# Retention queries and keys turned by DMA transposes of two 16-bit planes, in a two-layer decoder trunk

## The chip, the cores and the metric

The kernel runs on one core of a Trainium2 chip. The metric is the device time of the whole program in microseconds (us): the median of several runs, smaller is better. Beside the runs there is one profiled execution, whose trace lists every instruction of every engine: TensorE (PE in the rows; PEld are its weight loads), VectorE (DVE), ScalarE (ACT), GpSimd (POOL) and SyncE (SP; SPq is its queue of DMAs).

## What is computed

Two layers of a decoder trunk (`DEPTH = 2`), in float32, over 2048 prompt rows (16 tiles of 128) and 32 sample rows. Each layer has an attention head group (A) and a retention head group (B), whose outputs are gated, joined and projected back:

```python
h = rms_norm(x, norm_g);  p = einsum('ntd,de->nte', h, w_in)
qb = rotary(qb, pos, B_DK, theta_b);  kb = rotary(kb, pos, B_DK, theta_b) * B_DK ** -0.5
# retention, per chunk of 128 rows, B_HEADS = 4 heads, B_DK = B_DV = 128
scores = einsum('nihd,njhd->nhij', q, k) * decay
inner  = einsum('nhij,njhv->nihv', scores, v)
cross  = einsum('nihd,nhdv->nihv', q, S) * q_dec
S_new  = exp(lg * C) * S + einsum('njhd,njhv->nhdv', k * k_dec, v)
x = x + concat(silu(g_A) * A, silu(g_B) * rms_norm(inner + cross)) @ w_out
```

For `scores` and `cross` a product contracts over d, so the queries and keys of a tile, which lie in memory with one row of the sequence per partition, must be turned to have d on the partitions.

## The kernel before

A layer runs in four stages with the same 17 steps each, one per 128-row tile and one for the sample rows: A (projection of the attention columns, attention), B0 (projection and retention of heads 0 and 1), B1 (heads 2 and 3), O (the output projection). In the stages B0, B1 and O the steps are T0, T1, S (the sample rows), T2, 4, 5, ... up to F, the last one; a hardware loop runs most of them. The projections are float32 products made of three float16 products (high and low parts), 8 blocks of the contraction each. So one half of a step's projection (`proj`, L514) is 12 matmuls of 128x512, and a step has four such halves: two into one PSUM bank (queries and keys), two into the other (values and gate).

Each engine has a program of its own, written out in order; semaphores tie them together. In the stages B0 and B1 `step2` puts the retention of the tile before between the four halves of a tile's projection:

- after the first half: `b_T` (L657), four TensorE transposes of 128x128 float32 of the rotated queries and keys (`land[:, b, 0:512]`, two heads each) into PSUM bank `TK`;
- after the second: `b_ST` (L668), the scores, from `qkT`;
- after the third: `b_OS` (L687, L694, L703), outputs and state;
- after the fourth: nothing.

VectorE writes the rotated queries and keys in `b_rope` (L1162, L1170, L1171; it raises `b_qk`). It stands behind `b_decay` (L1182), which waits for the scores of the tile before. ScalarE copies the turned ones out of `TK` in `b_tout` (L1792, raises `b_te`, for which `b_ST` waits). It also makes the float16 weights of the next stage (`w_high`, L1657), the squares of the outputs (`b_squares`, L1799), and values and gate (`b_vg`, L1775 to L1779). SyncE's queue carries the mixed outputs to memory (`store_mix`, L2095), the sample states (`load_states`, L2110; stored at L2268), the DMA transposes of attention (`prob_T`, L2135), which turn 128x2048 numbers of float16 (512 KB) each, and in stage O those of the mixed rows (L2246) and of the next layer's input (L2252).

At the start of B0 the last attention tile, E, is still being worked on: `a_PV` of its two head groups stands after the third and the fourth half of B0's step T1, in front of `b_OS` of T0, and SyncE still has its two `prob_T` to issue.

Of the kernel before, what the change touches and what calls it, by code (L numbers as in the profile page):

```python
# [36 lines left out]
P = 128  # L37
# [133 lines left out]
def mid(c, i=0):  # L171

    return Step(c, i, SAMPLE_AT)
# [24 lines left out]
def trunk(nc, x_prompt, x_sample, cache_k, cache_v, state_ret, w_in, w_out, norm_g, q_g, k_g, sinks,  # L198
          rope_ap, rope_as, rope_bp, rope_bs, mask_a, mask_s, decay, decay_s, cols, ident,
          y_p, y_s, nk_p, nv_p, nst_p, nk_s, nv_s, nst_s, mixed):  # L200
    with ExitStack() as ctx:
# [70 lines left out]
        qkT = r2[:, 0:512]  # L272
        osq = r2[:, 640:896]
# [43 lines left out]
        b_qk, b_tk, b_te = sem("b_qk_ready"), sem("b_transposed"), sem("b_transposes_out")  # L317
# [58 lines left out]
        def all_h(eng, L):  # L376

            for p in range(2):
                eng.wait_ge(h_in[p], 16 * (L + 2) * (9 - p))

# [112 lines left out]
        def _(pe):  # L493
# [156 lines left out]
            def b_T(ph, L, s):  # L650

                b, r = lpar(ph, s), s.rows
                if ph == "B0" and s.fixed and s.c < 2:
                    pe.wait_ge(a_mx, 2 * (L + 1) * STEPS - 2 + 2 * s.c)
# [107 lines left out]
            def b_work(ph, L, s):  # L762
                return [[lambda: b_T(ph, L, s - 1)], [lambda: b_ST(ph, L, s - 1)],
                        [lambda: b_OS(ph, L, s - 1)], []]

            pe.wait_ge(id_ld, ID_LOADS * 16)
            def layer(L, last):
# [7 lines left out]
                with pe.Fori(0, (STEPS - 5) // 2) as i:  # L775
# [10 lines left out]
                    [lambda: b_T("B0", L, T0)],  # L786
# [3 lines left out]
                for ph in ("B0", "B1"):  # L790
# [5 lines left out]
                    b_T(ph, L, T1)  # L796
# [10 lines left out]
                step2("B1", L, F, [  # L807
                    [lambda: b_T("B1", L, F - 1)],
                    [lambda: b_ST("B1", L, F - 1)],
                    [lambda: b_OS("B1", L, F - 1)],  # L810
                    [lambda: b_T("B1", L, F)]])
# [837 lines left out]
        def _(act):  # L1649
# [132 lines left out]
            def b_tout(ph, L, s):  # L1782
                act.wait_ge(b_tk, bn(ph, L, s) + 1)
                if s.sample:
                    A.activation(qkT[:, 0:4 * NS], TK[:, 0:4 * NS], ACT.Copy)
# [81 lines left out]
            def layer(L, last):  # L1867
# [76 lines left out]
                F = mid(STEPS - 1)  # L1944
                b_vg("B0", L, T0)
                b_tout("B0", L, T0)
                b_vg("B0", L, T1)
                b_squares("B0", L, T0)

                def b_step(ph, s, k=None):  # L1950
                    nxt = "B1" if ph == "B0" else "O"
                    b_tout(ph, L, s - 1)
                    if k is not None:
                        w_high(L, nxt, k, 0)
                    b_squares(ph, L, s - 1)
# [4 lines left out]
                for ph in ("B0", "B1"):  # L1960
                    if ph == "B1":
                        b_tout("B0", L, F)
                        b_squares("B0", L, F)
# [6 lines left out]
                    b_tout(ph, L, S)  # L1970
                    act.wait_ge(b_mx, bn(ph, L, T1) + 1)
# [11 lines left out]
                b_tout("B1", L, F - 1)  # L1983
                b_squares("B1", L, F - 1)
# [90 lines left out]
        def _(sp):  # L2075
# [61 lines left out]

            def load_caches(L, which=(0, 1)):
# [238 lines left out]
```

## Time and profile before

| | us |
|---|---|
| median of 3 runs | 1932.44 (1929.9 to 1935.01) |
| profiled execution, first to last instruction (span) | 1923.8 |
| TensorE busy in it | 1790.1 (93%) |
| VectorE busy | 1385.0 (72%) |
| ScalarE busy | 721.9 (38%) |
| DMAs moved | 196.66 MB, mean 102 GB/s |

The span is what the trace shows; the median of the runs lies 8.6 us above it, for what lies around the first and the last instruction. Stage B0 of the first layer lies from about 385 to 606 us, B1 to 820 us, O to about 1010 us; in the second layer B0 begins at about 1312 us, B1 at 1533 and O at 1746 us.

### The profile page before, as it was taken

To read this page: it belongs to the slowest core of one execution; us is meant where nothing else is said; L and a number is where in the kernel's file an instruction comes from. 1 tells how busy PE (TensorE), PEld (TensorE's weight loads), DVE (VectorE), ACT (ScalarE), POOL (GpSimd) and SP (SyncE) were. 2 spreads that over 40 slices of the span, in tenths; PEclk is the share of its full clock that TensorE was granted. 3 is DMA by queue.
4 is the path that set the end of the run, shared out by engine and by line. 5 is a ranking of instruction groups with operands and counts; after the bars stand their busy time and mean duration, and the time that the engine had idled before them with its cause. 6 is when DMAs were issued, how large, how long until landed. Compare 5 with 4: busy or idle time off the path is not lost.

```text
span 1923.8 us, 35859 instructions
## 1 busy us (share of the span) xinstructions
PE 1790.1 (93%) x11752; PEld 989.6 (51%) x11752; DVE 1385.0 (72%) x4744; ACT 721.9 (38%) x1841; POOL 68.5 (4%) x108
## 2 busy tenths in 40 slices
PE   0778899999999999978998999999999999999999
PEld 0345555655555555533444655555555555555444
DVE  4769999977665766678885899998766576667442
ACT  2556576631232222232443556664123222222010
POOL 3010000010000000021001000000100000000000
PEclk9899999999999999989999999999999999999999
DMA  5874545463002100089994333335400021004875
GB/s 151 205 188 72 99 94 109 82 155 118 11 11 102 64 9 11 16 211 248 248 238 133 57 77 73 72 79 107 141 12 11 28 93 54 11 11 129 199 203 157
DMA packets 353806, 196.66 MB, mean 102 GB/s; under 512 B 296624, under 2 KB 327536, under 8 KB 353552
## 3 DMA queue, kind: packets, MB, share of 16 engines
q1 hardware_dynamic: 343984, 159.89, 35.5%
q0 software_dynamic: 9728, 35.66, 5.7%
q8 instruction: 42, 0.69, 0.1%
q14 instruction: 52, 0.43, 0.1%
HBM read 88.75 MB, written 41.16 MB: 68 GB/s over the span
## 4 chain that ended last, share of the span: by engine, by line
PE 58%; DVE 22%; DMA 6%; ACT 4%; issue 4%; SPq 2%; DVEq 0%; ACTq 0%; POOL 0%
PE PB L514 23%; PE PA L514 23%; DVE r L1060 2%; DMA r<-r 2%; DVE r L1017 2%; PE S L668 2%; PE OB L687 2%; PE TK L657 2%; PE S L703 1%; DVE mix L1135 1%; PE OB L694 1%; DVE r L1022 1%; DVE w_mx L871 1%; DMA out<-r 1%; ACT w_a L1727 1%
## 5 line engine op out<-in xcount | busy, mean ns | idle before, releaser
L514 PE MATMUL PB<-w_a,hT 128*128 128x512 f16 (+1 forms) x1920 | 404.4, 361 | 0.0
L514 PE MATMUL PA<-w_a,hT 128*128 128x512 f16 (+1 forms) x1920 | 403.0, 360 | 1.0 <-DVE land L1003 1.0
L514 PEld LDWEIGHTS PB<-w_a,hT 128*128 (+1 forms) x1920 | 185.7, 99 | 178.5 <-issue 11.8
L514 PEld LDWEIGHTS PA<-w_a,hT 128*128 (+1 forms) x1920 | 186.1, 99 | 171.4 <-issue 3.8
L514 PE MATMUL PA<-w_b,r 128*128 128x512 f16 x768 | 172.9, 382 | 20.4 <-DMA r<-r 15.3
L1799 ACT ACTIVATE r<-OB 128x128 f32<-128x128 f32 (+1 forms) x136 | 36.3, 272 | 390.7 <-PE S L703 364.2
L514 PE MATMUL PA<-w_b,hT 128*128 128x512 f16 x768 | 179.6, 384 | 0.0
L514 PE MATMUL PB<-w_b,hT 128*128 128x512 f16 x768 | 176.3, 379 | 0.6 <-DVE r L1162 0.6
L514 PE MATMUL PB<-w_b,r 128*128 128x512 f16 x768 | 171.3, 379 | 0.9 <-DVE r L1284 0.9
L1182 DVE TENSOR_TENSOR r<-S,t_dec 128x256 f32<-128x256 f32 x64 | 27.2, 425 | 156.1 <-PE S L668 155.9
L514 PEld LDWEIGHTS PA<-w_b,r 128*128 128x128 f16 x768 | 74.5, 98 | 115.0 <-DMA r<-r 20.5
L1727 ACT ACTIVATE r<-r,nm,unqk 128x256 f32<-128x256 f32 x192 | 112.6, 588 | 41.2 <-DVE sd L1073 41.2
L514 PEld LDWEIGHTS PB<-w_b,r 128*128 128x128 f16 x768 | 74.9, 98 | 91.2 <-DVE r L1284 2.2
L514 PEld LDWEIGHTS PA<-w_b,hT 128*128 (+1 forms) x768 | 75.4, 99 | 85.9 <-issue 6.4
L514 PEld LDWEIGHTS PB<-w_b,hT 128*128 (+1 forms) x768 | 74.8, 98 | 77.7 <-DVE r L1162 0.9
L1811 ACT ACTIVATE r<-r,minv 128x1024 f16<-128x1024 f32 (+1 forms) x34 | 39.1, 1149 | 142.2 <-DVE minv L1245 135.7
L1213 DVE SCALAR_TENSOR_TENSOR r<-r,S 128x128 f32<-128x128 f32 x120 | 29.1, 284 | 62.6 <-PE S L703 62.4
L540 PE MATMUL PA<-w_a,hT 128*32 128x256 f16 (+1 forms) x336 | 22.4, 345 | 54.4 <-DVE w_a L888 53.5
L1792 ACT ACTIVATE r<-TK 128x512 f32<-128x512 f32 x64 | 38.2, 596 | 77.6 <-PE TK L657 77.5
L1284 DVE SCALAR_TENSOR_TENSOR r<-PB,mdd,r 128x512 f32<-128x512 f32 x32 | 23.9, 748 | 56.7 <-PE PB L514 56.2
L1259 DVE SCALAR_TENSOR_TENSOR r<-r,minv 128x1024 f16<-128x1024 f32 (+1 forms) x34 | 43.5, 1278 | 16.5 <-ACT r L1811 16.4
L1657 ACT ACTIVATE w_b<-w_b,w_gs (+1 forms) x64 | 46.1, 720 | 16.1 <-DVE w_b L888 16.1
(258 smaller groups left out, 2894.3 us busy)
## 6 DMA issues: line engine op xcount, KB each, us to landing
out<-r SPq DMA_DIRECT2D x40, 512.0 KB, 4.7
r<-mixed SPq DMA_DIRECT2D x32, 512.0 KB, 4.1
w_b<-in_w_in POOLq DMA_DIRECT2D x16, 512.0 KB, 8.8
mixed<-mix SPq DMA_DIRECT2D x32, 256.0 KB, 2.0
mixed<-mix SPq DMA_DIRECT2D x64, 128.0 KB, 1.8
w_a<-in_w_in POOLq DMA_DIRECT2D x16, 512.0 KB, 8.0
w_b<-in_w_out POOLq DMA_DIRECT2D x16, 512.0 KB, 7.1
r<-in_x_prompt SPq DMA_DIRECT2D x16, 512.0 KB, 4.6
```

Source lines behind the costliest of these rows:

```text
L514: last = nc.tensor.matmul(out[0:s.rows, 0:n], lhs, w16(ph, k, p, wpart), start=(k == 0 and part == 0 and wpart == 0), stop=(k == KT - 1 an ...
L657: last = nc.tensor.transpose(TK[:, i * r:(i + 1) * r], land[0:r, b, i * P:(i + 1) * P], eye[0:r, 0:r])
L668: last = nc.tensor.matmul(S0[0:r, h * r:(h + 1) * r], qkT[:, (2 + h) * r:(3 + h) * r], qkT[:, h * r:(h + 1) * r], start=True, stop=True)
L687: nc.tensor.matmul(OB[0:r, h * P:(h + 1) * P], stm[0:r, h * r:(h + 1) * r], v, start=True, stop=s.first)
L1017: V.scalar_tensor_tensor(out=ph16[0][:, 1, :], in0=r1[:, 1536:2560], scalar=P_TOP, in1=ph16[0][:, 0, :], op0=ALU.mult, op1=ALU.subtract).t ...
L1060: return V.tensor_tensor_reduce(out=prob_q[g][h // 2][:, h % 2 * 256:h % 2 * 256 + 256], in0=(SS, XX)[g][h // 2][:, (h % 2) * 256:(h % 2) ...
L1259: V.scalar_tensor_tensor(out=m[0:r, 1, :], in0=mxt[0:r, b, :], scalar=minv[0:r, b:b + 1], in1=m[0:r, 0, :], op0=ALU.mult, op1=ALU.subtract ...
L1657: A.activation(w16(kind, k, c, 0), raw(L, kind, k, c), ACT.Copy, scale=w_gs[:, run(k, 1)]).then_inc(w_hi, 1)
L1727: A.activation(x, x, ACT.Exp, scale=unqk[:, 0:1], bias=nm[:, g, h:h + 1], accum_out=rsum[:, g, h:h + 1])
L1792: last = A.activation(qkT[:, :], TK[:, :], ACT.Copy)
L1799: last = A.activation(osq[0:r, h * P:(h + 1) * P], OB[0:r, h * P:(h + 1) * P], ACT.Square, accum_out=oss[0:r, h:h + 1])
L1811: A.activation(mh_of(s)[0:r, 0, :], mxt[0:r, b, :], ACT.Copy, scale=minv[0:r, b:b + 1]).then_inc(o_hi, 1)
```

## The change

In the tile steps of B0 and B1 the four TensorE transposes go (those of the sample rows stay). In their place:

1. `b_planes`, on ScalarE: when `b_rope` is done, it copies the 128x512 float32 of queries and keys as 1024 numbers of 16 bits into `pl`, the upper and the lower halves of the words apart.
2. `planes_T`, on SyncE: one DMA transpose of `pl` (128x1024 numbers of 16 bits, 256 KB) into `plT`, eight blocks of 128x128.
3. `b_tout`, on ScalarE: it waits for that transpose and joins the two planes into `qkT`.

`pl` and `plT` lie in columns of `w_a` that are free in these stages. `b_tout` also waits for `b_o`, the `b_OS` before, which read `qkT`.

```diff
+        pl = w_a[:, KT * N_B + SHIFT:KT * N_B + SHIFT + 512].bitcast(U16).rearrange("p (e n) -> p e n", e=2)
+        plT = w_a[:, KT * N_B + SHIFT + 512:KT * N_B + SHIFT + 1024].bitcast(U16).rearrange("p (e n) -> p e n", e=2)
...
             def b_work(ph, L, s):
-                return [[lambda: b_T(ph, L, s - 1)], [lambda: b_ST(ph, L, s - 1)],
-                        [lambda: b_OS(ph, L, s - 1)], []]
+                return [[], [lambda: b_ST(ph, L, s - 1)], [lambda: b_OS(ph, L, s - 1)], []]
...
             def b_tout(ph, L, s):
...
-                    last = A.activation(qkT[:, :], TK[:, :], ACT.Copy)
+                    act.wait_ge(b_pt, 16 * bt(ph, L, s) + 16)
+                    act.wait_ge(b_o, n)
+                    last = A.activation(qkT.bitcast(U16).rearrange("p (n e) -> p e n", e=2), plT, ACT.Copy)
                 last.then_inc(b_te, 1)
+
+            def b_planes(ph, L, s):
+
+                act.wait_ge(b_qk, bn(ph, L, s) + 1)
+                A.activation(pl, land[:, lpar(ph, s), 0:512].bitcast(U16).rearrange("p (n e) -> p e n", e=2),
+                             ACT.Copy).then_inc(b_pl, 1)
...
+            def planes_T(ph, L, s):
+
+                alone(sp, b_pl, bt(ph, L, s) + 1)
+                sp.dma_start_transpose(plT.rearrange("p e (c t) -> p (e c) t", t=P),
+                                       pl.rearrange("p e n -> p (e n)")).then_inc(b_pt, 16)
```

In the ordinary ScalarE step (`b_step` there) `b_planes` of a tile stands behind `b_tout` of the tile before, in front of `b_squares`. On SyncE `planes_T` of a tile stands in front of `store_mix` of the tile before.

TensorE, step T1 of the first layer's B0, before (TK is the bank of the transposes, S that of the scores, OB and TK at L644 are attention's outputs):

```order
L514 MATMUL PB<-w_b,hT 128x512 [waits dve_piece]
L514 MATMUL PB<-w_b,hT 128x512 x11
L657 MATMUL TK<-eye,land 128x128 [waits a_mixed,b_qk_ready]
L657 MATMUL TK<-eye,land 128x128 x3
L514 MATMUL PB<-w_b,hT 128x512 x12
L668 MATMUL S<-r 128x128 [waits b_transposes_out]
L668 MATMUL S<-r 128x128
L514 MATMUL PA<-w_b,hT 128x512 [waits dve_piece]
```

The same place with the change:

```order
L523 MATMUL PB<-w_b,hT 128x512 [waits dve_piece]
L523 MATMUL PB<-w_b,hT 128x512 x23
L675 MATMUL S<-r 128x128 [waits b_transposes_out]
L675 MATMUL S<-r 128x128
L523 MATMUL PA<-w_b,hT 128x512 [waits dve_piece]
```

The transposes and their two waits are gone, and the scores stand where they stood.

SyncE's queue from the end of attention into B0, first layer, before:

```order
L2135 DMA_TRANSPOSE r<-r 128x16x128 [waits a_probs_lo,a_pv]
L2224 DMA out<-land 128x128 x2
L2095 DMA mixed<-mix 128x512 [waits a_mixed]
L2135 DMA_TRANSPOSE r<-r 128x16x128 [waits a_probs_lo,a_pv]
L2095 DMA mixed<-mix 128x512 [waits a_mixed]
L2110 DMA r<-in_state_ret 128x8x128 [waits a_probsT_landed1,a_probsT_landed0]
L2110 DMA r<-in_state_ret 128x8x128
L2147 DMA qk_g<-in_q_norm_g 128x64
L2147 DMA qk_g<-in_k_norm_g 128x64
L2095 DMA mixed<-mix 128x256 [waits b_mixed] x2
```

With the change (`w_a<-w_a` is `planes_T`):

```order
L2247 DMA out<-land 128x128 x2
L2112 DMA mixed<-mix 128x512 [waits a_mixed]
L2152 DMA_TRANSPOSE r<-r 128x16x128 [waits a_probs_lo,a_pv]
L2158 DMA_TRANSPOSE w_a<-w_a 128x8x128 [waits b_planes]
L2112 DMA mixed<-mix 128x512 [waits a_mixed]
L2127 DMA r<-in_state_ret 128x8x128 [waits a_probsT_landed1,a_probsT_landed0]
L2127 DMA r<-in_state_ret 128x8x128
L2170 DMA qk_g<-in_q_norm_g 128x64
L2170 DMA qk_g<-in_k_norm_g 128x64
L2158 DMA_TRANSPOSE w_a<-w_a 128x8x128 [waits b_planes]
L2112 DMA mixed<-mix 128x256 [waits b_mixed] x2
```

The transpose of T0 comes behind attention's last one, that of T1 behind the last attention store, the two loads of states and, in the first layer, the two loads of gains.

ScalarE at the same place with the change (L1749 is the last row of attention; L1803 is `b_planes`, L1797 the join, L1776 to L1780 `b_vg`, L1810 `b_squares`):

```order
L1749 ACTIVATE r<-w_a 128x512
L1803 ACTIVATE w_a<-land 128x1024 [waits b_qk_ready]
L1776 ACTIVATE land<-PA,cs_B 128x256 [waits a_mixed,pe_piece]
L1778 ACTIVATE r<-PA,cs_B 128x128 x2
L1780 ACTIVATE land<-PA,cs_B 128x256
L1797 ACTIVATE r<-w_a 128x2x512 [waits b_out,b_planes_landed]
L1803 ACTIVATE w_a<-land 128x1024 [waits b_qk_ready]
L1776 ACTIVATE land<-PB,cs_B 128x256 [waits kv_out,a_mixed,pe_piece]
```

Before, these were the same rows without the two of L1803, and with one copy out of TK (L1792) in the place of the join.

## Rows read from the trace of the kernel before

**Rows 1.** Stretches B0, B1, B0, B1: us, each engine's busy time; PE clock; DMA.
```profile
core 0: us, PE busy (x) PEld busy (x) DVE busy (x) ACT busy (x) POOL busy (x), PEclk, DMA share, GB/s
384.00:595.00 211.00, 207.86 (x1283) 117.36 (x1281) 144.43 (x508) 61.65 (x194) 6.30 (x9) 0.99 0.24 68
595.00:828.00 233.00, 233.00 (x1339) 132.45 (x1338) 150.64 (x521) 58.71 (x184) 4.58 (x9) 0.99 0.14 46
```

**Rows 2.** Timeline, one loop step of B0: start us, duration us, engine, what.
```profile
507.76 0.60 PE L657 MATMUL TK<-eye,land 128*128 128x128 f32 x4
508.19 2.75 PE L514 MATMUL PA<-w_b,hT 128*128 128x512 f16 x12
513.55 0.42 DVE L1171 TENSOR_TENSOR land<-r 128x256 f32<-128x256 f32 x1
515.36 0.28 ACT L1799 ACTIVATE r<-OB 128x128 f32<-128x128 f32 x1 [5.76 <-PE S L703]
519.17 0.74 ACT L1657 ACTIVATE w_a<-w_a,w_gs  x1
523.36 0.61 PE L668 MATMUL S<-r 128*128 128x128 f32 x4
```

**Rows 3.** The transposes' line: count, duration ns min/median/max, first and last start.
```profile
L657 PE MATMUL TK<-eye,land x272: 221/273/331, 402.8 to 1745.8; 128*128 128x128 f32 x128, 32*128 32x32 f32 x8
```

**Rows 4.** Costliest groups, two ScalarE copies: busy us, mean ns | idle before.
```profile
L1792 ACT ACTIVATE r<-TK 128x512 f32<-128x512 f32 x64 | 38.2, 596 | 77.6 <-PE TK L657 77.5
L1743 ACT ACTIVATE r<-r 128x1024 f16<-128x1024 f32 x32 | 33.8, 1057 | 1.0
```

**Rows 5.** TensorE timeline, first layer's B0, steps T1 and T2.
```profile
402.80 0.63 PE L657 MATMUL TK<-eye,land 128*128 128x128 f32 x4 [0.79 <-DVE mix L1135]
405.85 0.61 PE L668 MATMUL S<-r 128*128 128x128 f32 x4
422.00 0.71 PE L668 MATMUL S<-r 128*128 128x128 f32 x4 [2.08 <-ACT r L1792]
422.55 4.44 PE L514 MATMUL PA<-w_b,hT 128*128 128x512 f16 x12
```

**Rows 6.** SyncE's queue, first layer, start of B0: start us, until the last is issued.
```profile
407.11 1.90 SPq L2135 DMA_TRANSPOSE r<-r  x1
414.79 2.21 SPq L2110 DMA_DIRECT2D r<-in_state_ret  x2
417.99 0.43 SPq L2147 DMA_DIRECT2D qk_g<-in_k_norm_g  x1
```

**Rows 7.** From issue to landing: all of L2135 and L2246, then 410 to 420 us, L2110.
```profile
DMA to landing us min/median/max: 2.5/4.4/9.8
...
DMA to landing us min/median/max: 4.8/5.4/6.0
```

**Rows 8.** Stretch in which L2135's data of 407.11 us move; columns as in rows 1.
```profile
410.00:410.50 0.50, 0.50 (x4) 0.25 (x3) 0.50 (x4) 0.00 (x0) 0.00 (x0) 1.00 1.17 217
```

**Rows 9.** Second layer, the same place: TensorE and SyncE's queue.
```profile
1332.86 0.61 PE L668 MATMUL S<-r 128*128 128x128 f32 x4
1349.55 2.75 PE L514 MATMUL PA<-w_b,hT 128*128 128x512 f16 x12
...
1333.77 1.88 SPq L2135 DMA_TRANSPOSE r<-r  x1
```

**Rows 10.** First layer's stage O: TensorE after a long wait, and the next half.
```profile
855.90 7.15 PE L514 MATMUL PA<-w_b,r 128*128 128x512 f16 x24 [9.66 <-DMA r<-r]
862.89 5.34 PE L514 MATMUL PB<-w_b,r 128*128 128x512 f16 x24
```

**Rows 11.** End of B1, first layer: TensorE and ScalarE.
```profile
823.22 0.71 PE L668 MATMUL S<-r 128*128 128x128 f32 x4
...
822.55 0.61 ACT L1792 ACTIVATE r<-TK 128x512 f32<-128x512 f32 x1
```

**Rows 12.** SyncE's queue, first layer's B0, around the sample states.
```profile
450.45 1.02 SPq L2110 DMA_DIRECT2D r<-in_state_ret  x2
```

More of the change, by code:

```diff
@@ L379, in all_h, with bt @@
                 eng.wait_ge(h_in[p], 16 * (L + 2) * (9 - p))
+        def bt(ph, L, s):
+            return (L * 2 + hb(ph)) * TILES + s.v - (0 if s.fixed and s.c < s.at else 1)
         def wn(L, kind):
@@ L1782, in b_tout @@
             def b_tout(ph, L, s):
-                act.wait_ge(b_tk, bn(ph, L, s) + 1)
+                n = bn(ph, L, s)
                 if s.sample:
+                    act.wait_ge(b_tk, L * 2 + hb(ph) + 1)
                     A.activation(qkT[:, 0:4 * NS], TK[:, 0:4 * NS], ACT.Copy)
@@ L1944, in layer @@
                 F = mid(STEPS - 1)
+                b_planes("B0", L, T0)
                 b_vg("B0", L, T0)
                 b_tout("B0", L, T0)
+                b_planes("B0", L, T1)
                 b_vg("B0", L, T1)
@@ L1954, in b_step @@
                         w_high(L, nxt, k, 0)
+                    b_planes(ph, L, s)
                     b_squares(ph, L, s - 1)
@@ L1970, in layer @@
                     b_tout(ph, L, S)
+                    b_planes(ph, L, T2)
                     act.wait_ge(b_mx, bn(ph, L, T1) + 1)
@@ L1983, in layer @@
                 b_tout("B1", L, F - 1)
+                b_planes("B1", L, F)
                 b_squares("B1", L, F - 1)
@@ L2227, in layer @@
                 prob_T(L, E, 1)
+                T0, T1, S, T2 = (mid(c) for c in range(4))
+                F = mid(STEPS - 1)
+                planes_T("B0", L, T0)
                 store_mix("A", L, E)
@@ L2233, in layer @@
                     load_gains(L + 1)
-                T0, T1, S, T2 = (mid(c) for c in range(4))
-                F = mid(STEPS - 1)
+                planes_T("B0", L, T1)
                 def mixed_T(s):
@@ L2256, in layer @@
                 for ph in ("B0", "B1"):
+                    if ph == "B1":
+                        planes_T("B1", L, T1)
                     store_mix(ph, L, T0)
                     store_mix(ph, L, T1)
+                    planes_T(ph, L, T2)
                     if ph == "B0" and L == 0:
@@ L2278, in layer @@
                         for c in (3, 4):
+                            planes_T(ph, L, mid(c + 1, i))
                             store_mix(ph, L, mid(c, i))
@@ L2282, in layer @@
                         load_mixed(L, S)
+                    planes_T(ph, L, F)
                     store_mix(ph, L, F - 1)
+                    if ph == "B0":
+                        planes_T("B1", L, T0)
                     if ph == "B1":
```

15 lines of the change are left out of this document (5 added, 10 removed).

## The prediction, on record before the result

> **What bounds the kernel now.** I read the busy time by stretches first, then the timeline of one loop step, then the two ends of the retention stages. In B1 TensorE is busy for all of 233.00 us, in B0 for 207.86 of 211.00; VectorE is at 65 to 68%, ScalarE at 25 to 29% [rows 1]. So in these stages time goes if TensorE work goes, and comes if TensorE waits. The few waits lie at the start of B0: 0.79 us before the first transposes, and 2.08 us before the scores of T1 [rows 5].
>
> **What goes.** One block of four transposes starts at 507.76 and the next projection matmul at 508.19: 0.43 us on TensorE [rows 2]. There are 64 such blocks (16 tiles, two stages, two layers; the row counts 272 with those of the samples, which stay [rows 3]). The engine's neighbours are projection matmuls that need nothing of them, so each block frees 0.43 us wherever nothing else is late. The mean of one is 273 ns [rows 3], but four take 0.43, because they overlap.
>
> The Trainium skill, page "TensorE: Matmul & The Clock Gate", section "Part 4: PE-mode transpose", gives some 275 ns for a transpose inside a kernel. The row's duration agrees with it and its spacing does not; counted by the page's figure, a block would be worth 1.1 us. That is a rival below.
>
> **What comes, and where it is covered: the loop.** Copy into planes: 1024 numbers, as L1743, 1.06 us; join: the same, against 0.60 for the copy it replaces [rows 4]. No row shows ScalarE taking every second 16-bit number; my ends are 0.60 us (the copy of 512) and 1.3 (an estimate, L1743 and a quarter), and I take 1.06, of the same count. The DMA: the 512 KB transposes land after 4.4 us [rows 7] and move at 217 GB/s [rows 8], so half of one is 1.2 us less: 3.2 us (ends: 2.5, the smallest landed, those of the 32-row tiles, and 4.4). Now in the clock of rows 2: rotation done 513.97, planes done 515.1, landed 518.4, ScalarE free of values, gate and weights at 519.9, join done 521.1. The scores stand at 523.36 less the 0.43 saved. So 1.9 us of slack, all behind ScalarE; the DMA alone could take until 521.8 and thus 6.6 us. The planes end before the squares' start at 515.36, so outputs, `b_mix` and gate stay in time. VectorE loses nothing: `b_decay` and `b_rope` wait for the scores as before. The bound stays TensorE, and every step is 0.43 us shorter. SyncE's `planes_T` waits in front of `store_mix` of the tile before, which becomes ready later anyway.
>
> That holds for all blocks but six: T0 and T1 of B0 and F of B1, in two layers. 58 x 0.43 = 24.9 us gained.
>
> **The start of B0, first wait.** The scores of T0 stand after the second half of step T1, at 405.85 [rows 5]. With the change they need the DMA transpose, and that stands on SyncE behind attention's last one, issued from 407.11 to 409.01 [rows 6]. The planes are ready by then: ScalarE had its copy out of TK done before the scores of 405.85, and one copy of 1.06 us more is still over before 409. Issue 409.1, landed 412.3, join and hand-offs 1.3: scores at 413.6, so 7.75 us later than before, and TensorE, which would be there at 404.6 (405.85 less 0.43 and the old wait of 0.79), waits 9 us. Nothing can pass: `a_PV` of tile E, the output of T0 and the rotation of T1 (behind `b_decay` on VectorE) all come after. In the second layer: SyncE free at 1335.65 [rows 9], scores at 1340.25 in place of 1332.86 [rows 9]: 7.4. Together 15.1.
>
> **The clock.** After a wait of 9.66 us in stage O, 24 matmuls took 7.15 us and the next 24 5.34 [rows 10]: the granted clock fell to 1.2 GHz for a while. A wait of 9 us here should cost the same 1.8 us, twice: 3.6.
>
> **Second wait.** The transpose of T1 is issued behind two state loads and, in the first layer, two gain loads, which are through at 418.4 [rows 6]. The second states are issued at 415.2 and land 6.0 us later [rows 7], at 421.2. Taking the transpose as landing 0.7 behind them, the join is done at 423.1 and the scores come at 423.2 in place of 422.00 [rows 5]: 1.2 us on top of the shift, in both layers (the loads are as long in the second). 2.4. In the first layer the clock fell there already (4.44 us for 12 matmuls [rows 5]), in the second not (2.75 [rows 9]); with a wait of 3.7 in place of 2.08 I charge one more fall, 1.7.
>
> The Trainium skill, page "DMA: Bandwidth & Descriptors", section "Queues, rings and completion order", says that each DMA engine takes a queue's descriptors in ring order. By that rule the transpose's data can't pass the states'; were it free to pass, it would land at 421.7 and the second wait would be some 0.2 us shorter, so the sum hardly hangs on it.
>
> **Two smaller places.** At the end of B1 the scores of F stood at 823.22, behind `b_tout` at 822.55 [rows 11], which waits for ScalarE's order (values, gate, mixed rows of stage O), not for data. The join is 0.5 us longer than the copy, so the step loses 0.5 where 0.43 was to gain: 1.0 for both layers. In step 4 of B0 the transpose is behind the states of B1, issued from 450.45 [rows 12]; in the first layer the cache copies, now issued 3 us later, push them. I get a join ending at about 459.1 with scores due at 459.2; I charge 0.5 (ends 0 and 2).
>
> **The sum.** -24.9 + 15.1 + 3.6 + 2.4 + 1.7 + 1.0 + 0.5 = -0.6 us. The profiled execution took 1923.8, and the median of runs is 8.6 above it: 1923.2 + 8.6 = 1931.8 us. A gain of 25 us in the loops is spent where the stages meet.
>
> **Rivals.**
> 1. Slower: the path rotation, planes, DMA, join does not shrink with size. It stands open in six places (T0, T1 and F, two layers) and nearly in step 4 of both stages. If a 256 KB transpose lands as late as a 512 KB one (4.4 in place of 3.2), that is 1.2 us at T0 and T1 (4.8), 0.4 at F (0.8), some 1.5 in the steps 4: 7.1 more, 1938.9 us; 1.3 us copies come to about the same. It decides from 0.8 us per pass, where the result is over 0.3% (5.8 us, about what a measurement of this kernel can tell from no change) slower. For it: the 32-row transposes still need 2.5 us, so most of a landing is no data; against it, the 1.2 us by the rate [rows 8].
> 2. Faster by a little: the clock doesn't fall after the two kinds of wait (5.3 us less), as it did not after the 2.08 us in the second layer [rows 9], and the landing is nearer 2.8: 1925 us. Against it is the 9.66 us row [rows 10].
> 3. Much faster: a transpose is worth its own 273 ns [rows 3], 58 x 1.09 = 63.3 in place of 24.9: 1893 us. The starts 507.76 and 508.19 speak against it.
> 4. Much slower: the loop becomes bound by the path. That needs a landing over 6.6 us in a quiet loop; at the slowest landed, 9.8 [rows 7], each of some 50 loop steps is 3.2 longer: 2090 us. In these loops the DMAs are nearly idle (share 0.14 to 0.24 [rows 1]), which speaks against it.
>
> **Chances.** Forecast, near no change, 0.51; rival 1 0.27; rival 2 0.15; rival 3 0.02; rival 4 0.05. Faster by over 0.3%: rivals 2 and 3 and an edge, 0.18; within 0.3% 0.50; slower 0.32. The range of 1924.5 to 1942 holds the forecast, rival 2 and rival 1 with one or two more falls of the clock.
>
> **What would show it.** TensorE's loop steps are 0.43 us shorter, with no idle time; ScalarE's groups of the two copies near 1.06 us, 64 each; `planes_T` landing near 3.2. At the start of B0 one TensorE wait of 9 us before the scores, put down to ScalarE's join, in each layer, and one near 3.7 a step later. I would be wrong if these waits are short (then 15 us and more faster), if the join ends after the scores are due in the loops, or if the clock falls in more places.

## The result, and the profile after

The changed kernel takes 1954.94 us (median, 1947.06 to 1961.46), the kernel before 1931.47 us beside it: a ratio of 1.012 (95% interval 1.0085 to 1.0156). A second set of six runs gave 1950.81 us against 1932.32, 1.0092 (1.0069 to 1.0115). So the change costs 18 to 23 us, where a difference of 0.6 us was forecast. The profiled execution of after has a span of 1945.3 us, against 1923.8 before. "Before", "after" and the other labels below name kernels; all intervals are 95%.

One thing that stands ahead of the prediction is to be put right here. The 8.6 us between the span before and the median of its runs are not all time around the first and the last instruction: every run lists its time and its span, and they differ by 1.8 us (1947.06 against 1945.3 for after). The rest is that the profiled execution before was a fast one: its mean granted clock is 0.984, where 47 runs of that kernel have 0.981 on average.

I read the same views as before, first the loops. TensorE's timeline, one loop step of B0, the scores of one tile and of the next:

```profile
506.49 0.61 PE L675 MATMUL S<-r 128*128 128x128 f32 x4
...
518.63 0.61 PE L675 MATMUL S<-r 128*128 128x128 f32 x4
```

The step is 12.14 us. Before, the same two scores were

```profile
510.79 0.61 PE L668 MATMUL S<-r 128*128 128x128 f32 x4
...
523.36 0.61 PE L668 MATMUL S<-r 128*128 128x128 f32 x4
```

so the step was 12.58 us (six steps in a row before 523.36 take 75.5), and the whole 0.43 us of the transposes is gained in each loop step, as forecast. ScalarE and SyncE in the same step:

```profile
509.70 1.06 ACT L1803 ACTIVATE w_a<-land 128x1024 uint16<-128x1024 uint16 x1 [4.50 <-DVE land L1172]
510.86 1.24 SPq L2158 DMA_TRANSPOSE w_a<-w_a  x1
...
515.50 1.36 ACT L1797 ACTIVATE r<-w_a 128x1024 uint16<-128x1024 uint16 x1
```

The planes' copy, the DMA and the join stand one behind the other. The join ends at 516.86 and the scores come at 518.63: 1.8 us of slack, where 1.9 were forecast.

The groups of the scores and of the two copies on the page and in the list of groups (busy us, mean ns, idle before with its releaser), and the landings of all 64 transposes by DMA:

```profile
L675 PE MATMUL S<-r 128*128 128x128 f32 (+1 forms) x272 | 44.2, 288 | 43.9 <-ACT r L1797 43.9
L1803 ACT ACTIVATE w_a<-land 128x1024 uint16<-128x1024 uint16 x64 | 67.6, 1057 | 289.2 <-DVE land L1172 289.2
L1797 ACT ACTIVATE r<-w_a 128x1024 uint16<-128x1024 uint16 x64 | 86.9, 1359 | 41.0 <-DMA w_a<-w_a 41.0
...
DMA to landing us min/median/max: 3.0/3.0/9.2
```

The 43.9 us are the result in one number: TensorE waits that long before scores, where it waited 5.7 before (two of 2.08 before the scores, two of 0.79 before the transposes, [rows 5] and their twins in the second layer). The copy into planes is as forecast, the join is 0.3 us longer than the 1.06 I took, and the landing is a little shorter than 3.2. The 43.9 us are in fifteen waits. TensorE's timeline, all of 1 us or more, and the 12 matmuls behind the two longest:

```profile
416.17 1.22 PE L675 MATMUL S<-r 128*128 128x128 f32 x4 [8.71 <-ACT r L1797]
417.18 5.26 PE L523 MATMUL PA<-w_b,hT 128*128 128x512 f16 x12
...
437.76 1.22 PE L675 MATMUL S<-r 128*128 128x128 f32 x4 [4.92 <-ACT r L1797]
...
480.63 1.22 PE L675 MATMUL S<-r 128*128 128x128 f32 x4 [4.37 <-ACT r L1797]
641.87 0.71 PE L675 MATMUL S<-r 128*128 128x128 f32 x4 [1.66 <-ACT r L1797]
692.58 0.71 PE L675 MATMUL S<-r 128*128 128x128 f32 x4 [2.13 <-ACT r L1797]
838.29 0.71 PE L675 MATMUL S<-r 128*128 128x128 f32 x4 [1.12 <-ACT r L1797]
1353.93 1.22 PE L675 MATMUL S<-r 128*128 128x128 f32 x4 [8.58 <-ACT r L1797]
1354.95 4.02 PE L523 MATMUL PA<-w_b,hT 128*128 128x512 f16 x12
1374.08 0.81 PE L675 MATMUL S<-r 128*128 128x128 f32 x4 [4.72 <-ACT r L1797]
1572.35 1.09 PE L675 MATMUL S<-r 128*128 128x128 f32 x4 [2.67 <-ACT r L1797]
1769.72 0.71 PE L675 MATMUL S<-r 128*128 128x128 f32 x4 [2.03 <-ACT r L1797]
```

In the order of the rows of the first layer: T0 and T1 of B0, step 4 of B0, T0 of B1, step 4 of B1, F; in the second layer T0 and T1 of B0, T0 of B1, F. The five left out are of 0.29 to 0.95 us, among them the last tile but one of B1 in each layer (0.95 and 0.94). None is in a quiet loop step; the scores of step 4 stand in the first pass of TensorE's loop, where SyncE is still busy with what went ahead of it.

By stages, worked out from the starts of each stage's first matmuls in the two profiled executions (forecast: the prediction's terms for that stage):

| stage | before, us | after, us | difference | forecast |
|---|---|---|---|---|
| A, layer 1 | 384.8 | 387.6 | +2.9 | 0 |
| B0, layer 1 | 221.0 | 235.1 | +14.1 | +5.2 |
| B1, layer 1 | 214.7 | 211.7 | -3.0 | -6.0 |
| O, layer 1 | 194.4 | 195.2 | +0.8 | 0 |
| A, layer 2 | 296.8 | 295.8 | -1.0 | 0 |
| B0, layer 2 | 221.1 | 226.8 | +5.6 | +6.1 |
| B1, layer 2 | 213.1 | 212.7 | -0.4 | -6.0 |
| O, layer 2 | 177.9 | 180.4 | +2.5 | 0 |

The 2.9 us of the first stage A aren't of the change: B0 begins at anything from 384.4 to 389.5 us in the thirteen profiles of this study, with the same work ahead of it. What was not forecast lies mostly in the retention stages, above all in the first B0 (8.9 us more than forecast) and the second B1 (5.6).

**SyncE's queue at the start of B0**, first layer, as in [rows 6]:

```profile
409.05 1.77 SPq L2152 DMA_TRANSPOSE r<-r  x1
410.94 1.90 SPq L2158 DMA_TRANSPOSE w_a<-w_a  x1
427.42 0.34 SPq L2112 DMA_DIRECT2D mixed<-mix  x1
427.88 1.25 SPq L2127 DMA_DIRECT2D r<-in_state_ret  x2
...
431.83 1.69 SPq L2158 DMA_TRANSPOSE w_a<-w_a  x1
```

The first transpose by DMA stands behind attention's last one, and the scores need it: the wait of 8.71 us. Attention's last tile, its product and its store then come late too (427.42), the states behind them, and behind these the transpose of T1: the wait of 4.92 us. Both are the waits that the prediction named.

**The clock** after the first wait, in stretches (us, PE busy, the other engines, PE clock, DMA share, GB/s):

```profile
418.00:420.00 2.00, 2.00 (x6) 0.76 (x5) 1.97 (x5) 0.00 (x1) 0.00 (x0) 0.50 0.00 0
...
424.00:426.00 2.00, 2.00 (x24) 1.12 (x22) 0.57 (x4) 0.00 (x0) 0.00 (x0) 1.00 0.01 4
```

The granted clock is 0.50, that is 1.2 GHz, until 422, so that 12 matmuls take 5.26 us in place of 2.75. In the second layer it rises sooner: the 12 matmuls behind the wait of 8.58 us take 4.02. Summing TensorE's busy time by (1 - granted clock) over the span gives the time lost to the lower clock: 23.3 us before, 36.8 after.

### The profile page after: what moved, and what is told of

It reads as the page before. It is cut to its first block, busy times and chain, and to the rows that moved or that the text cites. A ratio compares the mean times of both kernels' runs of the same rounds, so it can differ in the third digit from the quotient of the medians.

```text
span 1945.3 us, 35617 instructions
## 1 busy us (share of the span) xinstructions
PE 1776.1 (91%) x11496; PEld 963.7 (50%) x11496; DVE 1384.7 (71%) x4744; ACT 834.9 (43%) x1905; POOL 68.5 (4%) x108
## 4 chain that ended last, share of the span: by engine, by line
PE 50%; DVE 24%; DMA 9%; ACT 6%; issue 5%; SPq 3%; DVEq 0%; ACTq 0%; POOL 0%
PE PA L523 21%; PE PB L523 20%; DMA w_a<-w_a 3%; DVE r L1061 3%; PE S L675 2%; DMA r<-r 2%; DMA out<-r 2%; DVE r L1018 2%; PE OB L694 1%; DVE w_mx L872 1%; DVE r L1023 1%; DVE mix L1136 1%; PE S L710 1%; PE OB L701 1%; ACT r L1797 1%
## 5 line engine op out<-in xcount | busy, mean ns | idle before, releaser
L1803 ACT ACTIVATE w_a<-land 128x1024 uint16<-128x1024 uint16 x64 | 67.6, 1057 | 289.2 <-DVE land L1172 289.2
L523 PE MATMUL PA<-w_b,r 128*128 128x512 f16 x768 | 175.1, 386 | 17.7 <-DMA r<-r 15.7
L1797 ACT ACTIVATE r<-w_a 128x1024 uint16<-128x1024 uint16 x64 | 86.9, 1359 | 41.0 <-DMA w_a<-w_a 41.0
L675 PE MATMUL S<-r 128*128 128x128 f32 (+1 forms) x272 | 44.2, 288 | 43.9 <-ACT r L1797 43.9
L675 PEld LDWEIGHTS S<-r 128*128 128x128 f32 (+1 forms) x272 | 40.2, 196 | 60.0 <-ACT r L1797 51.3
L1810 ACT ACTIVATE r<-OB 128x128 f32<-128x128 f32 (+1 forms) x136 | 36.2, 272 | 71.9 <-PE S L710 51.6
```

The costliest lines, as they stand in the source:

```text
L523: last = nc.tensor.matmul(out[0:s.rows, 0:n], lhs, w16(ph, k, p, wpart), start=(k == 0 and part == 0 and wpart == 0), stop=(k == KT - 1 an ...
L675: last = nc.tensor.matmul(S0[0:r, h * r:(h + 1) * r], qkT[:, (2 + h) * r:(3 + h) * r], qkT[:, h * r:(h + 1) * r], start=True, stop=True)
L1797: last = A.activation(qkT.bitcast(U16).rearrange("p (n e) -> p e n", e=2), plT, ACT.Copy)
L1803: A.activation(pl, land[:, lpar(ph, s), 0:512].bitcast(U16).rearrange("p (n e) -> p e n", e=2), ACT.Copy).then_inc(b_pl, 1)
L1810: last = A.activation(osq[0:r, h * P:(h + 1) * P], OB[0:r, h * P:(h + 1) * P], ACT.Square, accum_out=oss[0:r, h:h + 1])
```

## Experiments

They are told in three sets, each of which ran on one chip beside the kernel before (1931.38, 1932.82 and 1932.32 us in them). `mid(0)`, `mid(1)`, `mid(16)` are T0, T1 and F.

**What is the removed TensorE work worth by itself?** Label notrans: no planes, no transpose; the join becomes a straight copy of the unturned rows, so its scores are not those of the reference.

```diff
-                    act.wait_ge(b_pt, 16 * bt(ph, L, s) + 16)
+                    act.wait_ge(b_qk, n + 1)
                     act.wait_ge(b_o, n)
-                    last = A.activation(qkT.bitcast(U16).rearrange("p (n e) -> p e n", e=2), plT, ACT.Copy)
+                    last = A.activation(qkT[:, :], land[:, lpar(ph, s), 0:512], ACT.Copy)
```

> This kernel is the changed one without the DMA transposes, without the copy into planes and without the join: ScalarE copies queries and keys unturned from land into qkT, so the scores are computed from unturned tiles (the transposing is left out, the rest of the work stays). It shows what the removed TensorE work alone is worth. Theory W (all that the change loses is TensorE waiting at the seams of the stages, and the clock falling after such waits): 64 x 0.43 = 27.5 us under the kernel before, 1904 us, TensorE idle time near that of before (132.8 us) and the time lost to the lower clock near that of before (23 us). Rival C (the clock is lower because TensorE has less to do between matmuls, waits or no waits): the loss to the clock stays near the 37 us of the changed kernel, and the time is 1914 us or more. Rival M (a transpose is worth more than its spacing): under 1895 us.

1905.78 us, ratio 0.9866 (0.9845 to 0.9887): 25.6 us under before; 64 blocks of 0.43 are 27.5. This bears out theory W: TensorE's idle time is 137.4 us and the loss to the clock 25.5. A transpose isn't worth its own duration.

**What does the DMA path cost by itself?** Label both: TensorE's four transposes are back in their old places (`b_T` of every tile), with nobody using them but the samples; the scores wait for planes, DMA and join.

> The changed kernel, with TensorE's transposes put back where they stood; nobody but the samples uses them, the scores still wait for the planes, the DMA and the join. The whole price of the DMA path, with the TensorE work kept. Theory W: 1954.9 + 27.5 for the transposes, less some 6.5 of the waits (15 waits, each absorbing one block of 0.43): 1976 us; loss to the clock again 33 to 37 us, because the waits are still there. Rival C (less TensorE work lowers the clock): with the work back the clock loss goes back to 23 us, 1963 us. The loops stand at 12.58 us per step as before under both.

1968.23 us, ratio 1.0212 (1.0179 to 1.0245), 37 us over before. It lies between the two numbers, nearer to C's. Its trace decides: the waits before the scores are 32.9 us, eleven less than in after where I had 6.5; those of 8.7 and 4.9 us are 7.97 and 4.53, and five of the small ones are gone. The loss to the clock stays at 33.5 us, as W has it, and is not the 23 of C. So less work on TensorE isn't what lowers the clock; that the waits are is borne out by the clocks of all the runs, behind the account below.

**Which tiles are it?** Label hyb_t0 gives T0 of B0 back to TensorE, hyb_b0 T0 and T1 of B0. In both a set names the steps that are turned the old way, and each of the three new operations (and `b_T` the other way round) asks it (`LOOP_DMA` is true here):

```diff
+        EX = {"B0": (0, 1), "B1": ()}
+        def by_dma(ph, s):
+            return not s.sample and ((s.fixed and s.c in EX[ph]) != LOOP_DMA)
...
             def planes_T(ph, L, s):
+                if not by_dma(ph, s):
+                    return
```

> The changed kernel with one tile of each layer, the first of B0, turned by TensorE as before; all others by DMA. Theory W: the waits of 8.71 and 8.58 us go (17.3), two falls of the clock with them (3.6 to 5), one block each comes back (0.9); the wait one step later stays at 3.5 to 5 because its transpose still stands behind the loads of the states: 1933 to 1936 us. Rival C: only the waits themselves go, 1938.5 us or more. Rival H (the wait is only handed on: with T0 early, T1 waits for the time that T0 did): over 1945 us, the second wait 8 us or more.

1931.23 us, ratio 0.9997 (0.9981 to 1.0012). Two of 64 tiles given back, and the loss is gone: theory W, with a little more than it asked. The wait at T1 is 5.85 and 4.70 us, 0.9 more than in after in the first layer and the same in the second, so the wait of T0 isn't handed on (rival H), and T1's transpose is late by its own place in SyncE's queue.

> The changed kernel with the first two tiles of B0 of each layer turned by TensorE as before. Theory W: all waits at the start of B0 go back to those of before (27.0 less 4), the clock loss in the two B0 stages back to that of before (11.0 to 3.5), four blocks come back (1.7): 1954.9 - 23 - 7.5 + 1.7 = 1926 us. Rival C: 1933 us or more, clock loss of the whole still over 30 us.

1923.59 us (ten runs, 1912.55 to 1930.91), ratio 0.9956 (0.9932 to 0.9981). Only the waits of before are left at the start of B0. The time is W's, and yet the loss to the clock in its profile is 33.0 us, as C says. By stages it isn't C's: of the 9.7 us more than before, 3.1 are in the first stage A and 1.6 in the second, where nothing is changed, 3.4 in the first B0 and B1, and 3.3 in stage O of the first layer, behind a wait:

```profile
858.62 7.50 PE L542 MATMUL PA<-w_b,r 128*128 128x512 f16 x24 [13.98 <-DMA r<-r]
```

That wait was there before, with 9.66 us [rows 10].

**The mirror of it.** Label only_t0: the kernel before, with T0 of B0 alone turned by DMA (the set names that step, and `LOOP_DMA` is false).

> The kernel before with a single tile of each layer, the first of B0, turned by DMA; the other 30 by TensorE as before. The price of one long wait by itself, twice. The wait should be 8.7 us as in the changed kernel, where the kernel before had 0.79, and one block less is done: 8.7 - 0.8 - 0.4 = 7.5 each, 15 for both. Theory F (a wait also costs a fall of the clock to 1.2 GHz for some 5 us of work after it, and a second one because T1's scores are late too): 3.6 to 8 us on top, 1950 to 1955 us. Rival N (the clock's falls are worth nothing that the comparison can see, since the kernel has others anyway): 15 us, 1946 us.

1950.27 us, ratio 1.0087 (1.006 to 1.0114): 18.0 us for two transposes out of 64, nearly the whole loss of the full change, and inside theory F's range. Its trace:

```profile
414.52 1.22 PE L698 MATMUL S<-r 128*128 128x128 f32 x4 [8.76 <-ACT r L1829]
415.54 5.14 PE L542 MATMUL PA<-w_b,hT 128*128 128x512 f16 x12
...
433.63 0.90 PE L698 MATMUL S<-r 128*128 128x128 f32 x4 [2.08 <-ACT r L1825]
434.33 4.29 PE L542 MATMUL PA<-w_b,hT 128*128 128x512 f16 x12
```

The 12 matmuls after the long wait lose 2.4 us (5.14 against 2.75) and the scores 0.5: 2.9 us for one fall of the clock, where I had charged 1.8. In the second layer the wait is 8.61 us, the 12 matmuls behind it take 3.81, and the fall costs 1.6. The fall after the wait of 2.08 us costs 1.5, and the kernel before has it too (4.44 us, [rows 5]). In this profile the two B0 stages together are 20.3 us longer than before.

**The waits that weren't forecast.** Label apart moves two transfers out of the way: the cache copies (`kc_out`) from the start of the first B0 to the end of its loop, and GpSimd's load of stage O's weights behind the transpose of T0 of B1:

```diff
                         if kind == "B1":
                             ...
+                        else:
+                            pool.wait_ge(b_pt, 16 * (bt("B1", L, mid(0)) + 1))
                         load_weights(G, kind, nl)
```

> The changed kernel with two transfers moved out of the way of its transposes: the cache copies are issued after the loop of the first B0 instead of at its start, and GpSimd loads the weights of stage O only once the transpose of the first tile of B1 has landed. Theory D (the waits that the forecast did not have come from transfers that stand or run ahead of the transpose): TensorE's wait before the scores of step 4 of the first B0 falls from 4.37 to under 1 us, those of the first tile of B1 from 1.66 and 2.67 to under 0.3, the long ones at the start of B0 stay (8.7, 8.6, 4.9, 4.7); 8.1 us of waiting and one fall of the clock less: 1944 to 1947 us. Rival P (these steps are bound by ScalarE's and SyncE's own order, not by transfers): the waits stay within 0.5 us, and the time stays 1955 us.

1941.35 us (ten runs), ratio 1.0047 (1.0025 to 1.007); after it stands at 1.0092 to 1.012. The waits are as theory D has them, the time is 3 us under its range. The wait of 4.37 us at step 4 and those of 1.66 and 2.67 at T0 of B1 are gone (nothing is left at either; the load, begun at 629.12 now, holds T1 of the first B1 for 0.81), and the four at the start of B0 stand at 8.76, 4.83, 8.62 and 4.63. What they were: in after, the transpose of step 4 is the last of these rows of SyncE's queue:

```profile
452.63 1.23 SPq L2158 DMA_TRANSPOSE w_a<-w_a  x1
453.91 1.53 SPq L2289 DMA_DIRECT2D out<-in_cache_swa_k  x2
455.48 1.30 SPq L2289 DMA_DIRECT2D out<-in_cache_swa_v  x2
461.38 1.02 SPq L2295 DMA_DIRECT2D out<-r  x2
464.79 2.32 SPq L2112 DMA_DIRECT2D mixed<-mix  x1
470.31 1.02 SPq L2127 DMA_DIRECT2D r<-in_state_ret  x2
471.64 2.77 SPq L2158 DMA_TRANSPOSE w_a<-w_a  x1
```

Copies, state stores and state loads each wait for those ahead, and the transpose for all. With the copies away it is issued at 466.98. And the transpose of T0 of B1 (632.27) ran beside the load of the weights for stage O, eight pieces of 512 KB issued from 625.33: it took 8.2 us to land (9.2 in the second layer), against 3.0 in the loops; in apart it lands after 3.1. Not forecast and not cured here are 1.92 us at step 4 of the first B1 and 0.95 at the last but one of both layers. Step 4 of B1 stands behind the loads of mixed rows (L2122) and of x (L2098), issued from 682.53, and its transpose landed after 7.05 us; in the second profile of after it landed after 4.84 and nothing waited.

**All seams at TensorE, the loops by DMA.** Label hyb_edge: `EX = {"B0": (0, 1), "B1": (0, 16)}`.

> Ten more steps towards the old way at the seams only: the first two tiles of B0 and the first and the last of B1 are turned by TensorE, in each layer, all others by DMA. Theory W: against the kernel with two tiles by TensorE (1923.6 us) the waits of 1.72, 1.35, 1.12 and 1.12 us go, four blocks of 0.43 come back: 1923.6 - 5.3 + 1.7 = 1920 us. Rival O (time won ahead of stage O of the first layer is lost again there, since TensorE's wait for the turned mixed rows, 10.2 us in the changed kernel, is 14.0 in the one with two tiles and 13.5 without any transposing): the waits of stage O grow by what the rest wins, 1923 to 1925 us.

1921.79 us (1913.56 to 1922.1), ratio 0.9939 (0.9917 to 0.9962): between the two theories. Its profile shows a wait of 15.87 us at the start of stage O of the first layer, and a loss to the clock of 30.9 us.

Label hyb_full: B1's last but one as well (step 15), the cache copies late, and SyncE's order turned around:

```diff
+                    planes_T(ph, L, mid(4))
                     for h in range(2):
                         sp.wait_ge(b_su, bn(ph, L, S) + 1)
...
-                    with sp.Fori(0, (STEPS - 5) // 2) as i:
+                    with sp.Fori(0, (STEPS - 7) // 2) as i:
                         for c in (3, 4):
-                            planes_T(ph, L, mid(c + 1, i))
                             store_mix(ph, L, mid(c, i))
+                            planes_T(ph, L, mid(c + 2, i))
```

> As the kernel with the tiles at the seams by TensorE, with the last but one of B1 as well; besides the cache copies are issued after the loop of the first B0, and SyncE issues each transpose one tile earlier in its row: that of step 4 ahead of the states, those of the loop ahead of the store of the mixed tile between. Theory W: no wait over 0.5 us before any scores but the 2.08 that the kernel before has too, so 54 blocks won at 0.43 (23 us): 1908 to 1912 us. Rival O (stage O of the first layer takes back what arrives early): 1912 to 1918 us. Rival Q (SyncE, waiting for planes, now holds back the stores and loads queued behind it, and the waits for them grow): over 1920 us.

1914.08 us (1909.06 to 1918.02), ratio 0.9916 (0.9898 to 0.9934): faster than both kernels, 18.7 us under before, with 54 of 64 tiles by DMA. The scores' group in the list:

```profile
L698 PE MATMUL S<-r 128*128 128x128 f32 (+1 forms) x272 | 40.9, 273 | 4.8 <-ACT r L1825 4.2 <-ACT r L1829 0.6
```

4.2 us are the waits of before, 0.6 are new. Rival Q is out; the time lies in the range that rival O has, 2 us over W's, and yet what rival O gives as the reason isn't in its profile: stage O's first wait is 10.02 us, and all of TensorE's idle time in that stage 19.2, against 19.6 before. On a guess at the cause of that wait I tried label hyb_spread, with GpSimd starting the next layer's weights two pieces later:

```diff
-                            pool.wait_ge(dve_piece, free + 1 + q)
+                            pool.wait_ge(dve_piece, free + 3 + q)
```

> The kernel with the tiles at the seams by TensorE and SyncE's new order, in which GpSimd also begins the weights of the next layer's stage A two pieces of stage O later, so that the first mixed rows of stage O are loaded and turned with fewer weights beside them. Theory E (TensorE's wait of 10 to 16 us at the start of stage O of the first layer is the turned mixed rows moving at the same time as these weights; DMA share 1.0 to 1.2 there): that wait falls by 4 us or more, one fall of the clock less perhaps, 1906 to 1911 us. Rival B (the same bytes are only moved later, into the next tiles' transposes, or VectorE waits for the weights): the sum of the waits in stage O stays within 2 us and the time is 1913 to 1918 us.

1919.45 us, ratio 0.993 (0.991 to 0.995), 5 to 6 us worse than hyb_full. The first wait of stage O is 11.42 us, and waits of 3.88 (for a DMA) and 7.29 (for VectorE) come after it; TensorE's idle time in the stage is 25.1 us against 19.2. Theory E fails, and it is also more than the 2 us and the 1918 us of rival B. What causes that wait, and what would shorten it, stays open.

**Why is the join longer?** Label contig writes its 16-bit numbers one behind the other:

```diff
-                    last = A.activation(qkT.bitcast(U16).rearrange("p (n e) -> p e n", e=2), plT, ACT.Copy)
+                    last = A.activation(qkT.bitcast(U16).rearrange("p (e n) -> p e n", e=2),
+                                        plT[:, 1:2, :].broadcast_to([P, 2, 512]), ACT.Copy)
```

> The changed kernel with a join that writes its 16-bit numbers one behind the other instead of every second one (it takes the high halves twice, so the scores are not those of the reference: the putting together is left out, the count of numbers copied is the same). Theory S (the 0.3 us by which the join exceeds the copy into planes is the price of writing every second 16-bit number): the join takes 1.06 us as the copy into planes does, and each wait before the scores at the seams is 0.3 us shorter. Rival R (the 0.3 us comes from reading what a DMA has just written, or from the place of the buffers): the join stays at 1.36 us.

```profile
L1797 ACT ACTIVATE r<-w_a 128x1024 uint16<-128x1024 uint16 x64 | 68.1, 1065 | 35.4 <-DMA w_a<-w_a 35.4
```

1065 ns in place of 1359: theory S. (The join also reads one plane twice in place of two planes; the numbers read still lie one behind the other.) The first waits of B0 are 8.37 and 8.24 us, 0.34 less each; of the second ones that of the first layer is shorter (4.50), that of the second is not (4.84 against 4.72). (One run, 1941.64 us.)

**The spread.** Label after_again, the changed kernel unchanged.

> The changed kernel once more, unchanged, for the spread of its times beside those of the other kernels of this set. If the four times seen (1947 to 1961 us) are typical, the median stays at 1950 to 1957 us and 1% or more above the kernel before; if the first three were high by chance, it comes to 1945 us.

1950.81 us (1944.85 to 1954.41): the loss is real, and the first set's median was at the high end. The waits before the scores were 40.8 us in this profile.

**The account of all of them.** Blocks not done on TensorE by 0.43 us, the change of the waits before scores and transposes against before's 5.7 us, and the change of the loss to the clock against before's 23.3 us, all from each kernel's own profile; beside it the difference of the medians, and that of the spans of the profiled executions themselves:

| kernel | tiles by DMA | blocks | waits | clock | sum | medians | spans |
|---|---|---|---|---|---|---|---|
| notrans | none turned | -27.5 | +1.6 | +2.2 | -23.7 | -25.6 | -18.7 |
| both | 64, TensorE too | 0 | +28.7 | +10.2 | +38.9 | +36.9 | +38.2 |
| only_t0 | 2 | -0.9 | +15.8 | +2.4 | +17.3 | +18.0 | +29.8 |
| after | 64 | -27.5 | +38.1 | +13.5 | +24.1 | +23.5 | +21.4 |
| after_again | 64 | -27.5 | +35.1 | +17.7 | +25.3 | +18.5 | +25.0 |
| apart | 64 | -27.5 | +29.5 | +5.6 | +7.6 | +8.5 | +11.7 |
| hyb_t0 | 62 | -26.7 | +18.9 | +7.4 | -0.4 | -0.2 | +12.4 |
| hyb_b0 | 60 | -25.8 | +12.3 | +9.7 | -3.8 | -7.8 | -1.5 |
| hyb_edge | 56 | -24.1 | +6.4 | +7.6 | -10.1 | -11.0 | -3.9 |
| hyb_full | 54 | -23.2 | +0.6 | +2.5 | -20.1 | -18.7 | -14.1 |
| hyb_spread | 54 | -23.2 | +0.6 | +10.3 | -12.3 | -12.9 | -3.6 |

For the change itself the account closes in the very executions that it is taken from: 24.1 us against a span longer by 21.4, and 25.3 against 25.0. Nothing else of the size of the loss has room there.

For the others it is looser than the medians make it look. Nine of eleven sums come within 2 us of the medians' difference, but their clock is that of a single execution, and against the spans of these same executions they are up to 13 us too low (hyb_t0, only_t0). What the sum leaves out is TensorE's idle time in the other stages, above all in stage O of the first layer: 27.9 us in hyb_t0 and 28.9 in only_t0, against 19.6 before. That the medians agree so well is in part luck.

On the clock there is more than the single profiles. Every run lists its mean granted clock: on average 0.981 in 47 runs of the kernel before, 0.974 in the ten of after, 0.977 in both, 0.983 in notrans and 0.982 in hyb_full. The kernels with few waits have the clock of before or more, whether TensorE has all of its transposes or none, and those with many waits have less. hyb_spread, with as few waits before scores as hyb_full and 6 us more of them in stage O, has 0.978.

## Why the prediction was wrong, step by step

**Right.** TensorE is the bound of the loops, a block is worth its spacing of 0.43 us and not 4 x 0.273 (notrans, and the loop steps), the path through planes, DMA and join is covered in the loops with 1.8 us to spare, the copy into planes takes 1.06 us. The first wait was forecast as 9 us in the first layer and 8.6 in the second, and measured 8.71 and 8.58. The mechanism is the one named; the closeness has some luck in it, since in the first layer the transpose was issued 1.0 us earlier after the start of B0 than I had taken and landed 0.6 us later (3.82 in place of 3.2). Luck is also in the whole stage B0 of the second layer, forecast as +6.1 and measured +5.6: the second wait there was 1.0 us longer than forecast, and the loss to the clock grew by 1.8 us where I had charged 3.5. Rivals 2, 3 and 4 did not happen.

**Wrong, "What goes", the 58 blocks without a wait.** The prediction let six tiles stand open and took all others for covered, because it had worked out one quiet loop step. There are five more at the seams of each layer: step 4 of both stages, T0 and T1 of B1, and the last but one of B1. For each I ought to have written out SyncE's queue and the other transfers at its place, as I did for T0 of B0:
- "Two smaller places", step 4 of B0: charged 0.5 us ("ends 0 and 2"), that is a wait of 0.9, measured 4.37. The prediction saw that the cache copies would push the states, and gave it too little: copies, stores, their landing, loads and then the transpose, each behind the one before. Counted from the scores of T1, the copies were issued 4.9 us later than before where I had 3, and the states 4.1; and the transpose took 7.6 us to land where the join that I "got" at 459.1 leaves it about 3. I had let it land behind the states at T1, and not here. Step 4 of B1: not charged, measured 2.13 and 0.50 (none and 0.24 in the second profile).
- T0 of B1: not in the prediction at all, measured 1.66 and 2.67, and 0.29 twice at T1. Its transpose meets the load of stage O's weights. apart shows this cause and that of step 4 of B0 by removing them: 8.6 us of waits and 9 to 14 us of time.
- The last two tiles of B1: for F a loss of 0.5 a layer where 0.43 was to gain, so a wait of 0.9, measured 1.12 and 2.03; for the one ahead nothing, measured 0.95 and 0.94. ScalarE turns to the mixed rows of stage O first (`o_mhi` ahead of the join), as the order of its program says. For F of the second layer that isn't all: its transpose stands behind that of the mixed rows and a load, landed after 4.7 us, and the join waited 0.80 us more for it.

**Wrong, "Second wait".** Forecast 3.7 us, measured 4.92 and 4.72: the states are held by attention's last store (427.42), which comes later by all of the first wait and the slow matmuls behind it, and the join is 0.3 us longer. Together 2.2 us more than forecast.

These terms add up: step 4 six us more than charged, T0 and T1 of B1 five, the last two tiles three, the second waits two, 16 in all. The forecast's waits were 9 and 8.6, twice 3.7, twice 0.9 and 0.9, together 28; TensorE waited 43.9. With the 8 us of the clock, next, that is the whole of the 24 us by which the forecast fell short.

**Wrong, "The clock".** I charged 1.8 us for a fall after a long wait, from a place in stage O [rows 10], and three falls in all, 5.3 us. In the first layer's B0 it costs 2.9 to 3.0 us (12 matmuls in 5.14 us in only_t0 and 5.26 in after, against 2.75, and 0.5 on the scores); in the second layer's it costs 1.6 and 1.8, as charged. And more waits brought more falls: 36.8 us lost against 23.3, 13.5 in place of 5.3. Of these 13.5 the first B0 has 5.3 and the first stage A, which isn't changed, 4.2; that part isn't owed to the change. The loss varies from run to run (41.0 us in the second profile of after), so I don't put it down tile by tile; why a fall costs 2.9 us in one place and 1.8 in another is open.

**The rival on the slower side** had the right places, six of them and "nearly in step 4 of both stages", and the wrong mechanism. It asked for a longer DMA landing in a quiet place (4.4 us in place of 3.2); the landing was 3.0 there. What was long were the landings in company, up to 9.2 us, and the queue ahead. The Trainium skill, page "DMA: Bandwidth & Descriptors", section "Queues, rings and completion order", says that a DMA engine consumes the descriptors of a queue in ring order; the prediction called that rule worth 0.2 us here. (By that section it is the landing that can't pass; it says that data may finish out of order.) The rows at step 4 of B0, where the transpose was issued 1.3 us behind the states and landed after 7.6 us (the join begins at 479.24) against 3.0 in a quiet step, fit the rule, and there more than 4 us hung on what stands ahead. They don't prove it: beside the weights that GpSimd loads through a queue of its own the transpose of T0 of B1 was as late (8.2 us), so that sharing the DMA engines is enough to explain both. No run tells the two apart.

**The range** of 1924.5 to 1942 was too narrow because every term had its ends, but the terms that I had not written had none. The profiled execution, which the sum was made against, was not the cause: the differences of the medians are as large.

## What to carry to other kernels

A change that frees the bound engine in a loop is paid for at the seams, where the new path has no neighbour to hide behind: two transposes out of 64 cost 18 us here, as much as 42 others gain. List every step outside the loop, write for each the queue and the transfers that stand or run ahead of the new operation, and count a wait with the fall of the clock behind it (here 8.7 us plus 1.6 to 3.0). Then leave the seams as they were: the mixed version, with 54 tiles by the new path and 10 by the old, beats the kernel before by 18.7 us and the changed one by 37 to 42, by the differences to the kernel before in each set.

## What the runs showed of the hardware

- ScalarE reads every second 16-bit number at the price of a plain copy (1057 ns for 1024 numbers per partition, against 1057 for the f16 copy of [rows 4]), but writing every second one costs 1359 ns against 1065 for the same count written one behind the other. The Trainium skill, page "SBUF — State Buffer", section "Door 1: The DMA port swizzle (why `[64,N]` ≈ `[32,N]`)", says of strides that accesses within the same 16-byte line hit full bandwidth; by that both should be free, and for the write the measurement differs.
- A 256 KB transpose by DMA lands after 3.0 us in a quiet stretch; after 4.8 to 7.1 us behind loads of mixed rows, 3.2 to 7.6 behind those of states, 8.2 to 9.4 beside a 4 MB load of weights (both profiles of after). The same instruction takes 1.24 us in SyncE's queue in a quiet step and up to 3.13 behind the states.
- TensorE's clock: after the wait of 8.7 us in the first layer the granted clock stood at 0.50 for 6.1 us of work (until 422.24), after that of 8.6 in the second for 3.6 (until 1357.49). After the wait of 2.08 us it fell in the first layer and not in the second of the same execution (4.44 against 2.75 us for 12 matmuls, [rows 5, 9]). The clock goes with the spread of equal runs: the ten of hyb_b0 span 18 us, the shortest (1912.55 us) with a mean granted clock of 0.987 and the longest (1930.91) with 0.977.
- In stage O of the first layer a wait for turned mixed rows was 9.1 to 18.6 us in the profiles of this study. It does not go by when a kernel gets there: TensorE began to wait at 832.8 us in notrans (13.5), 841.7 in hyb_full (10.0), 846.2 before (9.7), 857.9 in only_t0 (16.9) and 864.7 in both (9.1). So it is not shown that it takes back what is won ahead of it. Why it is sometimes short wasn't settled.
